# Low parts of y in y's own place, made at fixed steps beside the last input tiles; the residual in the normalised input's room

## What is computed

```python
h = rmsnorm(x, norm_w)
proj = jnp.einsum('bld,de->ble', h, w_in)
# ... three head groups give y_ssd, y_gdn, y_mem; z is the last part of proj
y = jnp.concatenate([headnorm(y_ssd), headnorm(y_gdn), headnorm(y_mem)], axis=-1)
y = y * mix_norm_w.astype(f32) * jax.nn.silu(z.astype(f32))
out = jnp.einsum('ble,ed->bld', y.astype(x.dtype), w_out)
return x + out            # a final rmsnorm follows
```

## Time and profile before

| | us |
|---|---|
| median of 3 runs | 1393.2 (1392.41 to 1394.38) |
| profiled execution, its own time | 1386.98 |
| its span, first to last instruction | 1385.2 |
| PE busy in the span | 1302.9 (94%) |
| VectorE, ScalarE, GpSimd busy | 713.5, 559.1, 431.3 |

### The profile page before, as it was taken

The page is one execution under the profiler, slowest core; times in us unless marked ns, Lnnn a source line. Parts: engine busy times, 40 slices in busy tenths (PEclk is TensorE's granted clock), DMA queues, the critical chain, the costliest instruction groups (busy, mean ns, idle before and its releaser), DMA issues.

```text
span 1385.2 us, 25241 instructions
## 1 busy us (share of the span) xinstructions
PE 1302.9 (94%) x10578; PEld 1240.6 (90%) x10578; DVE 713.5 (52%) x1025; ACT 559.1 (40%) x997; POOL 431.3 (31%) x405
## 2 busy tenths in 40 slices
PE   7999999899999999999999999999999979999993
PEld 6999998788899989898989889988889969999993
DVE  7764444555455656555564755397432362332224
ACT  6663333343435454545445354423223342222221
POOL 3030003232453434434452535573301150101003
PEclk9999999899999999999999999999999999999997
DMA  7334443111221111111211221366774324333323
GB/s 292 90 94 124 127 127 124 46 45 33 62 62 49 47 49 49 50 57 49 62 45 52 62 59 50 124 214 194 234 240 155 92 62 138 122 109 107 107 62 124
DMA packets 38816, 138.12 MB, mean 100 GB/s; under 512 B 4448, under 2 KB 5856, under 8 KB 38448
## 3 DMA queue, kind: packets, MB, share of 16 engines
q1 hardware_dynamic: 30384, 109.80, 25.8%
q10 hardware_dynamic: 8208, 26.22, 5.6%
q0 software_dynamic: 112, 0.50, 0.1%
HBM read 121.25 MB, written 15.24 MB: 99 GB/s over the span
## 4 chain that ended last, share of the span: by engine, by line
PE 69%; issue 10%; DVE 10%; POOL 4%; ACT 4%; DMA 2%; DVEq 0%; ACTq 0%; POOLq 0%; SPq 0%
PE ps L796 35%; PE ps L1123 16%; PE ps L688 12%; POOL w_lo L2061 2%; PE ps L744 2%; DVE conv_a L1693 2%; PE ps L748 2%; DMA out_s_ssd<-d_st 1%; DVE h_lo L1568 1%; ACT L1150 1%; DVE fin L2049 1%; ACT w_hi L1150 1%; DVE w_lo L1546 1%; POOL g_e L2127 1%; POOL s_l L2121 0%
## 5 line engine op out<-in xcount | busy, mean ns | idle before, releaser
L796 PE MATMUL ps<-h_hi,w_hi 128*128 128x260 f32 x1920 | 419.7, 300 | 16.6 <-DVE w_lo L1546 12.4
L796 PE MATMUL ps<-h_hi,w_lo 128*128 128x260 f32 x1920 | 388.1, 284 | 0.0
L796 PE MATMUL ps<-h_lo,w_hi 128*128 128x260 f32 x1920 | 388.0, 284 | 0.0
L1150 ACT ACTIVATE w_hi<-w_raw 128x512 fp32r<-128x512 f32 x352 | 212.9, 624 | 400.3 <-PE ps L796 194.3
L796 PEld LDWEIGHTS ps<-h_hi,w_hi 128*128 128x128 f32 x1920 | 299.2, 191 | 36.9 <-issue 31.4
L796 PEld LDWEIGHTS ps<-h_lo,w_hi 128*128 128x128 f32 x1920 | 298.1, 190 | 0.0
L796 PEld LDWEIGHTS ps<-h_hi,w_lo 128*128 128x128 f32 x1920 | 298.0, 190 | 0.0
L1546 DVE TENSOR_TENSOR w_lo<-w_raw,w_hi 128x512 fp32r<-128x512 f32 x216 | 157.2, 749 | 258.2 <-ACT w_hi L1150 257.9
L2061 POOL TENSOR_TENSOR w_lo<-w_raw,w_hi 128x512 fp32r<-128x512 f32 x136 | 180.2, 1328 | 253.0 <-ACT w_hi L1150 252.5
L1123 PE MATMUL ps<-y_hi,w_hi 128*128 128x260 f32 x640 | 129.0, 283 | 9.6 <-DVE y_lo L2033 5.6
L1123 PE MATMUL ps<-y_lo,w_hi 128*128 128x260 f32 x640 | 129.2, 283 | 0.0
(11 more groups left out here) (372 smaller groups left out, 1776.6 us busy)
## 6 DMA issues: line engine op xcount, KB each, us to landing
w_raw<-in_w_in SPq DMA_DIRECT2D x120, 512.0 KB, 3.6
w_raw<-in_w_out SPq DMA_DIRECT2D x40, 512.0 KB, 3.6
w_raw<-in_w_mem SPq DMA_DIRECT2D x16, 512.0 KB, 3.6
x_t<-in_x_t SPq DMA_DIRECT2D x8, 520.0 KB, 7.6
fin<-in_x_t SPq DMA_DIRECT2D x8, 520.0 KB, 4.5
out_y_t<-fin SPq DMA_DIRECT2D x8, 520.0 KB, 2.7
d_st<-in_st_ssd ACTq DMA_DIRECT2D x8, 512.0 KB, 4.8
out_s_ssd<-d_st ACTq DMA_DIRECT2D x8, 512.0 KB, 5.3
```

What stands on the lines that cost most here:

```text
L796: last = mm(out[:, hf, :], w[:, g % 2, P * (at_k % 8):P * (at_k % 8) + P], a[:, at_k, HALF * hf:HALF * hf + HALF], start=(at_k == 0 and j ...
L1150: return nc.scalar.activation(out, in_, func, **more)
```

## The change

Three things. `y_lo` takes the place of `y_raw`: the subtraction of block e writes over the block that it reads, and the waits of the first low parts on the last input matmul go. `fin` and the small tiles beside it move to `r_h`; SyncE loads its first pieces at step 6 of the first output tile, behind a wait for the last input matmul. And the splits of y move in the order: for blocks 0 to 18 the high part stands at step 222 + 2.4 e (265 + 2 (e - 16) from block 16 on) and the low part 1.6 steps later, among the last input tiles. The decode gate of blocks 16 to 19 is cut in two, blocks 16 to 18 at step 264.5, and block 19. After the last input tile the five items of tile 59, the decode gate of block 19 and its two parts stand between the output steps 0 to 7.

```diff
...
-           (207.4, "ysq"), (208.8, "yss"), (210, "yln"), (212, "ynorm"), (216, ("gate", 0)), (218, ("gate", 1))]
+           (207.4, "ysq"), (208.8, "yss"), (210, "yln"), (212, "ynorm"), (216, ("gate", 0)), (218, ("gate", 1)), (264.5, ("gate", 2))]
...
-                    ("dec_gated", 6)],
+                    ("dec_gated", 8)],
...
-    for it in proj_items(b, NTILE - 1):
+    for e in range(ET - 1):
+        start = 222 + 2.4 * e if e < 16 else 265 + 2 * (e - 16)
+        for step, name in ((start, "yhi"), (start + 1.6, "ylo")):
+            at_step = PHASE * GDN_H + step
+            phases.setdefault(int(np.floor(at_step)), []).append((at_step, (name, e)))
+    for it in proj_items(b, NTILE):
         items.append(it)
         if it[0] == "proj":
             items += [g for _, g in sorted(phases.pop(KT * (it[1] - b) + it[2], []), key=lambda x: x[0])]
     assert not phases
-    items += spread(proj_items(NTILE - 1, NTILE), [("yhi", e) for e in range(ET - 4)])
-
-    items += [("ylo", 0), ("ylo", 1), ("post", NTILE - 1, 0), ("post", NTILE - 1, 1), ("post", NTILE - 1, 2), ("ylo", 2), ("ylo", 3), ("out", 0, 0), ("post", NTILE - 1, 3),
-              ("out", 0, 1), ("post", NTILE - 1, 4), ("out", 0, 2), ("dec", "gate", 2), ("ylo", 4), ("ylo", 5)]
-    items += spread([("out", 0, e) for e in (3, 4, 5)], [("yhi", e) for e in range(ET - 4, ET)])
+    last = NTILE - 1
+    for it in (("post", last, 0), ("out", 0, 0), ("post", last, 1), ("out", 0, 1), ("out", 0, 2), ("post", last, 2), ("out", 0, 3), ("post", last, 3),
+               ("out", 0, 4), ("post", last, 4), ("dec", "gate", 3), ("out", 0, 5), ("out", 0, 6), ("yhi", ET - 1), ("out", 0, 7), ("ylo", ET - 1)):
+        items.append(it)
     for n in range(KT):
         for e in range(ET):
-            if n == 0 and e < 6:
+            if n == 0 and e < 8:
                 continue
-            if n == 0:
-                items.append(("ylo", e))
             items.append(("out", n, e))
...
     y_hi = r_side.place("y_hi", [P, ET, NT], F32R)
-    y_lo = at("y_lo", [P, ET, NT], F32R, r_h.start)
-    fin = at("fin", [P, KT, NT], F32, r_y.start)
-    r_h.reset(r_h.start + ET * NT * 4)
+    y_lo = at("y_lo", [P, ET, NT], F32R, r_y.start)
+    r_h.reset()
+    fin = r_h.place("fin", [P, KT, NT])
     fin_w = r_h.place("fin_w", [P, KT])
...
             if it in ring:
...
-            if k == "out" and it[1] == 0 and it[2] == ET - 1:
-
-                spe.wait_ge(*upto("y_hi_done", ET))
-                spe.wait_ge(*upto("y_lo_g", ET // 2))
-                spe.wait_ge(*upto("y_lo_v", ET // 2))
+            if k == "out" and it[1] == 0 and it[2] == 6:
+
+                spe.wait_ge(*upto("unit_used", in_units))
                 spe.dma_start(fin_w[:, :], I["final_w"]).then_inc(sem("fin_w_in"), 16)
                 load_residual(0)
                 load_residual(1)
...
                 if e == 0:
...
-                if e in (0, 8, 16):
-                    act.wait_ge(*upto("dec_gated", 2 * (e // 8 + 1)))
+                if e in (0, 8, 16, 19):
+                    act.wait_ge(*upto("dec_gated", 2 * ((0, 8, 16, 19).index(e) + 1)))
...
             elif k == "out" and unit_of(it)[1] in (0, 3):
...
                 elif step == "gate":
                     part = it[2]
-                    e0, e1 = ((0, 8), (8, 16), (16, 20))[part]
+                    e0, e1 = ((0, 8), (8, 16), (16, 19), (19, 20))[part]
...
             elif k == "ylo" and it[1] % 2 == 1:
                 e = it[1]
-                if e == 1:
-                    dve.wait_ge(*upto("unit_used", in_units))
...
             elif k == "out" and unit_of(it)[1] in (2, 5):
...
             elif k == "ylo" and it[1] % 2 == 0:
                 e = it[1]
-                if e == 0:
-                    pool.wait_ge(*upto("unit_used", in_units))
...
```

## The result

| | before | after |
|---|---|---|
| median, first runs (4 each) | 1392.81 us (1386.75 to 1394.38) | 1374.73 us (1372.66 to 1377.53) |
| ratio after to before | | 0.9879 (95% interval 0.9844 to 0.9915) |
| profiled execution, its span | 1386.98, 1385.2 us | 1377.53, 1375.4 us |
| all executions timed later | 84, median 1388.9 (1382.5 to 1395.6) | 19, median 1377.3 (1371.1 to 1381.9) |

The account below looks back on a forecast made before the run. The prediction took TensorE, busy 94% of the span, as the bound, with an 11.40 us hole before output step 19. Its sum, -11.40 + 0.3 = -11.1 us off 1393.2, gave 1382.1 us, range 1380.3 to 1386.0.

Parts of the forecast that it names:

- The hole: PE's waits for low parts of y, between the last input tile and output step 19; closing it gains 11.40 us.
- Met waits cost nothing: Output steps' waits met long ahead cost nothing visible; six steps already pass the same waits at 0.72 us each.
- Cost beside the input tiles: Low parts moved beside the last input tiles make weight halves late: 0.3 us, with 0 and 2.5 as ends.
- sum with the rule of the Trainium skill: Beside the last input tiles, VectorE and GpSimd pass the port in turn: 2.4 us late in 6.2 units, 1384.2 us.
- Step 8: Second output weight unit, needed by 1123.9 us: its second low half ends at 1123.1, spare 0.8 us, cost taken as 0.
- Residual: Earlier residual load into h's room: the first residual add's 3.62 us data wait goes, but that gives nothing.
- (a): Weight halves become late beside the last input tiles or at step 8: 2.5 to 5 us back, middle 1385.6; chance 0.12.
- (c): The stall only moves: some low part is not ready, keeping half of the gap, 5.7 us: 1387.5 us; chance 0.06.
- (b): VectorE becomes the bound beside the last input tiles, each operation waiting for GpSimd: 23 us late, 1404.8 us; chance 0.04.
- the last line of the sum: Whole kernel: the 11.1 us gain taken off 1393.2 us, the median of the runs shown, giving 1382.1 us.
- (d): PE gains beyond 11.4 us through a shorter tail or better clock; clock said to stand at 1.00: 1380 us; chance 0.04.

Follow-up runs that it names:

- doubled: Changed kernel with each of low parts 0 to 18 made twice, first into a scratch tile, its engine waiting on the result: 1387.66 us, 0.9993 to the kernel before.
- crowded kernel: Changed kernel with the high and low parts of blocks 0 to 15 crowded into 15 steps instead of 36: 1384.18 us, 0.9977 to the kernel before.
- filling: Changed kernel with idle matmuls before five PE waits: 1372.16 us, 0.9871 to the kernel before, output wrong; mended, 1373.48 us, 0.9897.
- before, again: The kernel before, unedited, timed against itself: 1389.42 us against 1388.41, ratio 0.9996.
- rooms alone: Kernel before with only the new places of y_lo and fin, without the first low parts' waits on the last input matmul, old order: 1387.95 us, 0.9996.

## Why the prediction was wrong

*The hole: right.* Forecast 11.40 us, H fell by 11.43, to 13.90 (forecast 13.93: 13.7 from the first output step, and the 0.24 in front of it). *Met waits cost nothing: right.* *Cost beside the input tiles, 0.3 us, 0 to 2.5: 0* in every profile of the changed kernel; lateness begins not far from there, as the doubled and the crowded kernel show. The prediction's sum with the rule of the Trainium skill on the shared port ("SBUF — State Buffer", section "Who interferes with whom") gave 2.4 us. The trace agrees with the lock, as two operations that meet take 1.7 to 1.8 us; the lateness isn't there. In the profile of the changed kernel VectorE was idle before the first weight half of every unit from 1083 us on, for at least 0.64 us and waiting for ScalarE, so that no lateness passed from one unit to the next, and at most one low part stood between the two halves of a unit. The shortest of these pauses:

```profile
1092.21 1.09 DVE L1546 TENSOR_TENSOR w_lo<-w_raw,w_hi 128x512 fp32r<-128x512 f32 x1 [0.64 <-ACT w_hi L1150]
```

The sum had every operation of a unit in front of PE's need; those behind the second half are not.

*Step 8:* forecast spare 0.8, measured 1.2. *Residual:* nothing, and nothing measured. *Rivals:* (a) and (c) did not happen; (b) needs about twice the low parts; there its mechanism shows, at some 10 us in place of its 23.

*The step that failed is the last line of the sum.* It took 11.1 us off 1393.2, a median of three, and allowed 1 us of scatter, for which it gave no row. That median is not where the kernel before stands: of its 84 later executions 11 are at 1392.4 or above, the lowest of those three, and the middle is 1388.9. Off that middle the same gain gives 1377.8; the middle of the 19 later ones of after is 1377.3. The sum against the profile's own time, which the prediction also made, gave 1375.9 for the changed execution, and 1377.53 came. The 6.2 us between profile and median were taken as a property of the timing; they lie within the scatter of 13 us that the later executions show, and in the profiles that scatter is in P alone. It could have been seen: the runs and the profile of before already differed by 6 us, and its page shows a clock under 1.00 at 242 to 277 us, the eighth of 40 slices (each digit is tenths of full speed, 9 being 90% or more):

```profile
PEclk9999999899999999999999999999999999999997
```

With the scatter as measured, a median of four has no business in a range of 5.7 us; and the statement that a measurement tells 0.2%, 2.8 us, holds only for many executions: the interval of the first four against four, 0.9844 to 0.9915, is 0.7% wide. The four first executions of after were at the quick end too (1372.7 to 1377.5 of 1371.1 to 1381.9), so both medians erred away from each other, by 3.9 and 2.6 us: 18.1 instead of 11.6. That is partly luck, but three out of three as high as 11 of 84 would be rare by luck alone; whether something else held the first executions of before high stays open, since their clock is not on record.

The Trainium skill, "TensorE: Matmul & The Clock Gate", part 1, section "What's actually happening", says that the chip judges PE's activity in windows that run free of the kernel, so that the same kernel meets them differently from run to run. The traces agree as far as they go: the wait near 243 us is 2.66 or 2.67 us in each profile without filling, and the clock in the ten microseconds around it is 0.83 in one (after) and 0.77, with 0.89 in the next ten, in another (before, again):

```profile
240.00:250.00 10.00, 6.53 (x34) 0.77 0.16 52
250.00:260.00 10.00, 9.37 (x70) 0.89 0.18 53
```

The prediction had read the clock only where the change was: its rival (d) says that the clock stood at 1.00 throughout, which its rows show from 1060 us on.

## What to carry to other kernels

Work that several engines make in a burst between two PE stages belongs beside the stage before, as soon as its place in memory permits; give its room first, then its steps, and check each engine's queue for what PE waits for behind it. Spread such work so that VectorE and GpSimd don't meet in every operation: engines that were to be 62% and 55% busy by the sum, and were 64% and 57% from 1082 to 1118 us, had 0.7 us to spare. And before a range is written, see how far single executions lie apart and where the clock falls: the hole was sized to 0.1 us and the forecast missed by the base it was taken from.

## What was not expected of the hardware

A long wait of PE was paid twice in two kernels. The crowded kernel lost 10.2 us of clock up to 1110 us, as much as the first profile of after, and its P is 5.9 us later, for one wait of 4.44 us. Behind the wait the clock fell; PE's table by stretch of the crowded kernel:

```profile
1110.00:1115.00 5.00, 4.17 (x35) 1.00 0.09 37
1115.00:1120.00 5.00, 1.39 (x6) 0.81 0.17 17
1120.00:1125.00 5.00, 5.00 (x38) 0.85 0.23 91
```

and of the doubled one, where PE came back at 0.50, about the lower of the two clock levels, 1.2 GHz:

```profile
1095.00:1100.00 5.00, 0.71 (x6) 0.98 0.00 0
1100.00:1105.00 5.00, 3.19 (x15) 0.50 0.37 105
1105.00:1110.00 5.00, 5.00 (x37) 0.84 0.38 110
```

The hole of before, 9.6 us idle in pauses of up to 2.13 us, kept 1.00, while a single wait of 2.66 us brought 0.83. But neither the sum nor the longest pause decides it. In the profile of the rooms alone the hole is shorter, 7.1 us idle from 1118.2 to 1144 in pauses of up to 2.10 us, and there the clock fell:

```profile
1120.00:1130.00 10.00, 5.25 (x37) 0.96 0.12 47
1130.00:1140.00 10.00, 7.71 (x54) 0.87 0.19 57
```

What makes the difference from one execution to the next stays open. And matmuls that do nothing useful, 62 of them in five waits, made the kernel some 4 us faster.
